# A decoder step with linear attention and window softmax: gate chain of the next tile moved into the output product, and scores as three half-precision passes

## What is computed

```
u = rmsnorm(x) * norm_in
gq, gk, gv, g_gate, g_low, sq, sk, sv, s_gate = split(u @ w_in)
log_a = log_sigmoid(g_low @ w_gate_up + b_gate) / 16           # per token and feature
o_gla[t] = q_t S_t,   S_t = diag(exp(log_a_t)) S_{t-1} + k_t v_t^T   # 4 heads of 64 x 128
p = softmax([q k^T / 8 over the last 128 tokens, sink])         # 8 query heads of 64, 2 key heads
o_swa = p v
y = rmsnorm(x + concat(rmsnorm(o_gla) * silu(g_gate), o_swa * silu(s_gate)) @ w_out) * norm_f
```

## Time and profile before

| | |
|---|---|
| median of 3 runs | 964.44 us (964.41 to 966.28) |
| the profiled execution | 965.73 us, span 963.9 us |
| PE busy | 890.4 us, 92% of the span |
| DVE busy | 693.7 us, 72% |
| ACT busy | 399.4 us, 41% |
| POOL busy | 98.4 us, 10% |
| mean granted clock of PE | 0.958 of 2.4 GHz |

### The profile page before, as it was taken

How to read it: one execution, slowest core, us unless ns; L and a number is a source line. 1 busy time by engine, 2 the same in 40 slices (tenths; PEclk the granted TensorE clock), 3 DMA queues, 4 the chain that set the end, 5 groups by cost and what they waited for, 6 DMA issues and landing times.

```text
span 963.9 us, 21703 instructions
## 1 busy us (share of the span) xinstructions
PE 890.4 (92%) x8701; PEld 619.6 (64%) x8701; DVE 693.7 (72%) x2124; ACT 399.4 (41%) x1096; POOL 98.4 (10%) x125
## 2 busy tenths in 40 slices
PE   1597689999999999999999999999999999999977
PEld 1583357585857667675758585766757575856755
DVE  5999858576685949585857768594958586776673
ACT  6786434343424344343434342434434343433311
POOL 1455101010100001010101010000101010101000
PEclk9799699999999999999999999999999999997776
DMA  9640102020202001020202020200102020101220
GB/s 378 239 176 1 66 1 88 1 90 1 89 1 88 3 35 54 1 89 1 89 1 89 1 88 1 89 2 33 58 2 88 1 89 1 48 2 45 80 109 24
DMA packets 15219, 56.47 MB, mean 59 GB/s; under 512 B 3569, under 2 KB 5001, under 8 KB 13840
## 3 DMA queue, kind: packets, MB, share of 16 engines
q1 hardware_dynamic: 14832, 55.02, 15.1%
q10 hardware_dynamic: 288, 0.07, 0.0%
HBM read 44.30 MB, written 10.78 MB: 57 GB/s over the span
## 4 chain that ended last, share of the span: by engine, by line
PE 71%; DVE 21%; ACT 3%; issue 3%; DMA 1%; SPq 0%; DVEq 0%
PE bank L516 19%; PE bank L517 18%; PE bank L518 18%; DVE flex L1413 4%; PE bank L667 3%; DVE bank L1407 2%; PE bank L601 2%; DVE flex L409 2%; PE bank L714 2%; PE bank L691 1%; PE bank L687 1%; DMA w_out_lo<-in_w 1%; DVE flex L1318 1%; PE bank L653 1%; DVE flex L408 1%
## 5 line engine op out<-in xcount | busy, mean ns | idle before, releaser
L516 PE MATMUL bank<-u_hi,w_in_hi_lo 128*128 128x128 f16 (+1 forms) x1288 | 209.7, 215 | 14.1 <-DVE w_in_hi_lo L1557 13.9
L517 PE MATMUL bank<-u_lo,w_in_hi_lo 128*128 128x128 f16 (+1 forms) x1288 | 209.4, 215 | 0.0
L518 PE MATMUL bank<-u_hi,w_in_hi_lo 128*128 128x128 f16 (+1 forms) x1288 | 209.4, 215 | 0.0
L516 PE MATMUL bank<-w_in_hi_lo,u_hi 128*128 128x512 f16 (+3 forms) x528 | 176.9, 343 | 1.1 <-ACT win_q L970 0.9
L517 PE MATMUL bank<-w_in_hi_lo,u_hi 128*128 128x512 f16 (+3 forms) x528 | 176.6, 343 | 0.0
L518 PE MATMUL bank<-w_in_hi_lo,u_lo 128*128 128x512 f16 (+3 forms) x528 | 176.6, 343 | 0.0
L516 PEld LDWEIGHTS bank<-u_hi,w_in_hi_lo 128*128 128x128 f16 x1288 | 124.6, 99 | 26.2 <-DVE w_in_hi_lo L1557 14.0
L517 PEld LDWEIGHTS bank<-u_lo,w_in_hi_lo 128*128 128x128 f16 x1288 | 124.5, 99 | 0.2
L518 PEld LDWEIGHTS bank<-u_hi,w_in_hi_lo 128*128 128x128 f16 x1288 | 124.5, 99 | 0.0
L516 PE MATMUL bank<-w_out_hi,ogT_hi 128*128 128x512 f16 x256 | 98.0, 383 | 0.0
L517 PE MATMUL bank<-w_out_lo,ogT_hi 128*128 128x512 f16 x256 | 98.0, 383 | 0.0
(11 more groups left out here) (270 smaller groups left out, 1811.1 us busy)
## 6 DMA issues: line engine op xcount, KB each, us to landing
xT<-in_xT SPq DMA_DIRECT2D x16, 512.0 KB, 4.5
x_rows<-in_xq SPq DMA_DIRECT2D x16, 512.0 KB
flex<-in_w SPq DMA_DIRECT2D x4, 2048.0 KB, 9.9
flex<-in_xq SPq DMA_DIRECT2D x16, 512.0 KB, 3.6
out_y<-flex SPq DMA_DIRECT2D x16, 512.0 KB, 2.6
w_out_lo<-in_w SPq DMA_DIRECT2D x2, 2048.0 KB, 10.1
w_out_hi<-in_w SPq DMA_DIRECT2D x1, 2048.0 KB, 10.2
w_out_hi<-in_w SPq DMA_DIRECT2D x1, 1088.0 KB, 7.2
```

What stands on the lines that cost most here:

```text
L516: nc.tensor.matmul(out, a_hi, b_hi, start=start and i == 0, stop=False)
L517: nc.tensor.matmul(out, a_hi, b_lo, start=False, stop=False)
L518: mm = nc.tensor.matmul(out, a_lo, b_hi, start=False, stop=stop and i == last)
```

## The change

Scores: queries and keys are kept as high and low 16-bit halves (`q16`, `k16`), and each score product is three half-precision matmuls that add up in PSUM (hi*hi, hi*lo, lo*hi). ACT writes the queries' high half from PSUM, DVE the low half (new `take_sq`), and DVE now frees the bank. DVE writes both halves of the keys. The scale is no longer applied to queries and keys but in `row_max`, where the immediate -1 becomes a per-partition scalar `nsig` made in the prologue. The keys to be returned are scaled apart (`k_last`).

Gate chain: of tile t+1 in iteration t. `turn_low` and `gate_up` stand before and behind the first part of `proj gg`; the order of the ring `tr` follows. `take_z` stands behind `take_gv`, `log_gate` behind `head_norm`, `sums` and then `split_v` behind `norm_x`, `decays` ahead of ACT's `split_u`, `factors` between `residual` and `final_norm`, POOL's `differences` at the end of its iteration. Tile 0 has its own copies of the first steps. In the last tile, ahead of which the sample tokens are projected, none of it is left. In the prologue ACT's `take_sq` of tiles 0 and 1 moves to rounds 3 and 4 and DVE gets its part in the same rounds.

```diff
         pj = Ring(banks[0:2], ...
-                  [("bc", "dve"), ("gqk", "act"), ("sq", "act"), ("sklow", "dve"), ("gv", "dve"),
+                  [("bc", "dve"), ("gqk", "act"), ("sq", "dve"), ("sklow", "dve"), ("gv", "dve"),
         tr = Ring(banks[4:6], ...
-                  [("glT", "act"), ("z", "dve"), ("pt0", "dve"), ("pt1", "dve"), ("pt2", "dve"), ("pt3", "dve"),
-                   ("KST", "act"), ("SU", "dve"), ("og0", "dve"), ("og1", "dve")])
+                  [("pt0", "dve"), ("pt1", "dve"), ("pt2", "dve"), ("pt3", "dve"), ("KST", "act"),
+                   ("glT", "act"), ("z", "dve"), ("SU", "dve"), ("og0", "dve"), ("og1", "dve")],
...
 # scores (PE)
                 for i in range(2):
-                    for h, name in enumerate(units):
-                        mm = nc.tensor.matmul(..., sq[r:r + HD, t.p, 2 * pair + i, :], kwin[r:r + HD, t.p, :],
-                                              start=True, stop=True)
+                    for step, (lq, lk) in enumerate(((0, 0), (0, 1), (1, 0))):
+                        for h, name in enumerate(units):
+                            mm = nc.tensor.matmul(..., q16[r:r + HD, t.p, lq, 2 * pair + i, :],
+                                                  k16[r:r + HD, t.p, lk, :], start=step == 0, stop=step == 2)
 # take_sq (ACT), take_sq (DVE, new)
+                    nc.scalar.activation(q16[:, t.p, 0], bank, ACT.Identity, scale=V_UNIT).then_inc(act_q.sem, 1)
+            def take_sq(t):
+                act_q.wait(dve, "qh", t)
+                V.scalar_tensor_tensor(out=q16[:, t.p, 1], in0=pj.bank("sq", t)[:, :].rearrange(
+                    "p (f c) -> p f c", f=GRP), scalar=V_UNIT, in1=q16[:, t.p, 0], op0=ALU.mult, op1=ALU.subtract
+                                       ).then_inc(pj.freed["dve"], 1)
 # take_kv (DVE)
-                    V.tensor_scalar(kwin[:, t.p, P:2 * P], bank[:, 0:P], inv[:, 2:3], None, ALU.mult)
+                    V.tensor_scalar(k[:, 0, P:2 * P], bank[:, 0:P], V_UNIT, None, ALU.mult).then_inc(dve_k.sem, 1)
                     V.tensor_scalar(vf[:, t.p, :], bank[:, P:2 * P], V_UNIT, None, ALU.mult)
+                    dve_k.wait(dve, "kh", t)
+                    V.scalar_tensor_tensor(out=k[:, 1, P:2 * P], in0=bank[:, 0:P], scalar=V_UNIT,
+                                           in1=k[:, 0, P:2 * P], op0=ALU.mult, op1=ALU.subtract)
 # row_max (DVE)
-                    m = V.tensor_tensor_reduce(..., band[:, first], -1.0,
+                    m = V.tensor_tensor_reduce(..., band[:, first], nsig[:, :],
 # PE, iteration
                 if not early:
-                    turn_low(t)
                     proj(nxt, "gqk")
-                    gate_up(t)
                     scores(t, 0)
...
                 turn_keys(t)
+                turn_low(t)
                 if early:
                     proj_rest(nxt, "gg", 6)
                 else:
                     proj(nxt, "gg", 3)
+                gate_up(t)
                 gla_out(t)
 # ACT, prologue and iteration
-                if i == 5:
-                    take_sq(Tile(1))
                 if i == 3:
                     take_qk(Tile(1))
+                    take_sq(Tile(0))
                 if i == 4:
-                    take_sq(Tile(0))
+                    take_sq(Tile(1))
...
-                decays(t)
                 probs(t, 2)
...
                 take_kst(t)
+                take_low(t)
                 head_norm(t)
+                log_gate(nxt)
                 take_out(t, 0)
...
                 nc.scalar.preload_act_table_set(LOG_EXP_SET)
+                decays(nxt)
                 split_u(t + 2)
 # DVE, prologue and iteration
+                    V.tensor_scalar(nsig[:, :], invq[:, 1:2], inv[:, 2:3], -1.0 / (V_UNIT * V_UNIT), ALU.mult, ALU.mult
+                                    ).then_inc(scored, 1)
+                    dve.wait_ge(scored, 1)
+                    V.tensor_scalar(nsig[:, :], nsig[:, :], -SCORE_FLOOR, None, ALU.min)
+                if i == 3:
+                    take_sq(Tile(0))
                 if i == 4:
+                    take_sq(Tile(1))
                     take_gv(Tile(0))
...
-                take_z(t)
                 row_max(t, 0)
                 row_max(t, 1)
-                sums(t)
+                take_sq(nxt)
                 take_pt(t, 0)
                 take_pt(t, 1)
                 row_max(t, 2)
                 row_max(t, 3)
-                factors(t)
                 take_pt(t, 2)
                 take_kv(nxt)
...
                 take_gv(nxt)
-                split_v(nxt)
+                take_z(t)
                 mean_square(t + 2)
                 gate_window(t)
...
                 norm_x(t + 2)
+                sums(nxt)
+                split_v(nxt)
                 scale_u(t + 2)
                 split_u(t + 2)
                 residual(t)
+                factors(nxt)
                 final_norm(t)
```

More of the change, by code:

```diff
@@ L114, with __init__ @@
 class Ring:
-    def __init__(self, banks, full, freed, order, tail=None, head=None):
+    def __init__(self, banks, full, freed, order, tail=None, head=None, last=None):
         self.banks, self.full, self.freed, self.order = banks, full, freed, order
+        self.last = order if last is None else last
         self.tail = order if tail is None else tail
@@ L126, in _list @@
     def _list(self, t):
+        if t.static and t.off == NT - 1:
+            return self.last
         return self.tail if t.sample else self.order
@@ L235, in hymba_step_kernel @@
         bsum = part(FT * P).rearrange("p (f c) -> p f c", f=FT)
+        KST = part(HG * DK)
+        k_last = part(P)
         assert at[0] <= 8192
@@ L616, in values @@
             def values(t, u):
-                if u == 0 and not (t.static and t.off == 0):
-                    dve_o.wait(pe, "sg", t + -1)
+                if u == 0:
+                    if t.static and t.off == 0:
+                        pe.wait_ge(z_taken, 1)
+                    else:
+                        dve_o.wait(pe, "sg", t + -1)
                 if u == 0:
@@ L643, in gate_up, with first_turn_low, first_gate_up @@
                 mm.then_inc(tr.full, 1)
+            def first_turn_low():
+                pj.wait_freed(pe, "sklow", Tile(0))
+                nc.tensor.transpose(accS[0:RANK, 0:P], glow[:, 0, :], ident[:, :]).then_inc(low_turned, 1)
+            def first_gate_up():
+                pe.wait_ge(low_taken, 1)
+                for f in range(FT):
+                    mm = nc.tensor.matmul(accS[:, (f + 1) * P:(f + 2) * P], wgu[:, f * P:f * P + P], glT[:, :],
+                                          start=True, stop=True)
+                mm.then_inc(z_full, 1)
             def leaf_scores(t):
@@ L969, in take_sq @@
                 bank = pj.bank("sq", t)[:, :].rearrange("p (f c) -> p f c", f=4)
-                nc.scalar.activation(sq[:, t.p, :, 0:n], bank[:, :, 0:n], ACT.Identity,
-                                     scale=invq[:, 1:2]).then_inc(pj.freed["act"], 1)
+                if t.sample:
+                    nc.scalar.activation(s_q[:, :, 0:n], bank[:, :, 0:n], ACT.Identity,
+                                         scale=invq[:, 1:2]).then_inc(pj.freed["act"], 1)
+                else:
+                    nc.scalar.activation(q16[:, t.p, 0], bank, ACT.Identity, scale=V_UNIT).then_inc(act_q.sem, 1)
             def take_gate(t, g):
@@ L1157, in body @@
                 early = t.static and t.off == 0
-                if not early:
-                    take_low(t)
+                if early:
+                    log_gate(t)
+                else:
                     take_qk(nxt)
-                log_gate(t)
                 probs(t, 0)
@@ L1175, in body @@
                     probs_hi(t, 1)
-                decays(t)
+                if early:
+                    decays(t)
                 probs(t, 2)
@@ L1746, in _ @@
                     dve.wait_ge(w_lo_pool, i)
-                    take_z(Tile(0))
+                    first_take_z()
                     row_max(Tile(0), 0)
@@ L1783, in body @@
                 early = t.static and t.off == 0
-                if not early:
-                    take_z(t)
+                if early:
+                    sums(t)
+                else:
                     row_max(t, 0)
                     row_max(t, 1)
-                sums(t)
+                if not early:
+                    take_sq(nxt)
                 take_pt(t, 0)
```

84 lines of the change are left out of this document (56 added, 28 removed).

## The result

The changed kernel takes **971.69 us** (median of 5 runs, 971.61 to 976.64) against 965.44 for the kernel before on the same chip: ratio 1.0088, interval 1.0074 to 1.0102. (The ratio takes in all runs, the two long ones too; the medians alone stand at 1.0065.) It is slower, as forecast, but by 6.2 us in the median instead of 2.6. 971.69 is within the outer range of 962.0 to 972.5, outside the forecast's own range of 964.5 to 970.5, and close to the 971.3 of rival (a).

A forecast was written before the change was run, and what follows sets the result against it. TensorE was taken as the bound, busy over nine tenths of the span; prologue +3.7, tile 0 +0.8, steady tiles -0.8 and tail -1.1 gave +2.6, 967.0 us as a median; own range 964.5 to 970.5, outer range 962.0 to 972.5.

The forecast's parts named there:

- rival (a): Prologue: PE's clock falls in the idle before gv of tile 1, +4.3 us more, 971.3 us; chance 0.2.
- The split takes the sums' place; the wait does not go: Steady tile, before the last transposes: DVE's query split replaces the sums; PE's wait grows about 0.45 to some 1.1 us.
- Rival (b): Steady tile: the wait goes after all, tile 51.1, 950 us; milder form 962.5; together chance 0.14.
- I take 0: Row maximum on DVE: a second per-partition scalar costs between 0 and 0.06 us per instruction, four on the path; taken as 0.
- One more change of rows: Steady tile, gate-up moved behind the hole on PE: one added change of rows, 0.09 us of the 0.84 moved.
- Cover enough by a hair: Tile boundary: ACT's second exponential ends at about 11.65, when PE asks for it at 11.69.
- Scores: Steady tile on PE: twelve half-precision matmuls with overlapping heads take 0.75 us, 0.31 less than before.
- Rival (d): Scores: the half-precision heads do not overlap, +9 us, 976 us; chance 0.06.
- Prologue +3.7: Prologue: DVE's split of tile 1's queries holds up PE's gv of tile 1, +3.7 us, bounds +1.1 and +8.5.
- Rival (c): Prologue: it hides its new work and PE's gv is not held up, 964.5 us; chance 0.10.
- Tile 0 +0.8: Tile 0: it takes gate-up of tile 1 on board, +0.8 us.
- Tail -1.1: Last tile, to the start of the sample's gv: 13.4 instead of 14.5 us, set by DVE, -1.1 us.

The follow-up runs named there:

- e2: Changed kernel with single-precision queries, keys and scores as before, so the gate chain's move alone: 965.64 us, ratio 1.0007.
- e1: Changed kernel with the immediate -1 back in the row maximum and the scores left without their scale: 969.89 us, ratio 1.0049.
- e9: Changed kernel with late query split, early leaf scores, prologue statements moved, scale in the query and key splits, immediate -1 in the row maximum: 947.86 us, ratio 0.9818.
- e4: Changed kernel with three prologue statements moved: ACT's tile 0 query copy later, DVE's tile 1 query split earlier: 968.45 us, ratio 1.0037.
- e3: Kernel before with the three-pass scores alone, gate chain in its old place, query split behind the sums: 1000.4 us, ratio 1.0367.
- e11: Kernel before with three-pass scores alone, query split behind the fourth row maximum on DVE and behind the probabilities on ACT: 990.52 us, ratio 1.0260.

## Why the prediction was right and where it failed

- **The split takes the sums' place; the wait does not go.** Right, and its size was close (1.15 us against "some 1.1"). The stretch that holds it came out 0.16 longer than forecast: 0.25 more for the row maxima, 0.09 less for ACT's copy. Rival (b) is out with it. What the forecast did not see is that before the change ACT's copy of the queries already stood just behind the sums, which e2 shows.
- **"I take 0" for the second per-partition scalar.** The step that failed. It measures 0.061 for each of the instructions, the upper bound that I had from the earlier trace rows. The reason given, that the instruction already fetches one, was an argument and no row. Four of them are on the path: 0.25 a tile, 3.4 us in all; taking the scalar away gave back 0.23 a tile (e1). The forecast's median was 4.7 us too low (3.6 in the difference to the kernel before), and this term is the greater part of it.
- **"One more change of rows" for gate-up.** It costs two, it seems: the scores kept theirs, and gate-up, once between `gqk` and the scores, now needs one on each side. `gg`'s three steps take 2.03 instead of 1.94, and the first matmuls of the output 0.97 instead of 0.86. 0.1 us a tile too little, 1.3 in all. No run isolates it. ACT's copy with an immediate scale (0.60 us, against 0.69 for the old one; e9 shows that it is the scale) gave back 0.09.
- **"Cover enough by a hair"** at the boundary: it was gone by a hair. The first four transposes take 0.69 us instead of 0.61; that costs nothing that shows in the changed kernel, but e9 shows that it counts once the hole is closed.
- **Scores** at 0.75 us with overlapping heads: 0.76. Rival (d) falls.
- **Prologue +3.7:** +3.9, by the waits named; only the bound step of DVE came at 82.99 instead of 80.2, as `gv` took longer. Rival (c) is out. **Tile 0 +0.8:** 1.0 without the clock. **Tail -1.1:** -0.56 to the sample's `gv` and -0.61 behind it, under other low stretches of the clock. With the same code there, e4's last tile takes 12.98 us instead of 13.85, 1.4 less than before, so this stage moves by 0.9 with the low stretches that fall into it.
- **Rival (a)** came true in the profiled run: 2.5 us instead of 4.3, as the clock came back during `gv`. What I held against it, that the fall in the earlier trace rows came late in its hole, was a poor argument from one case. That its 971.3 lies so near the median of 971.69 is luck: the account below reaches the median without that fall, by the tiles, and the profiled run, which has it, took 976.64. The rule of the Trainium skill ("TensorE: Matmul & The Clock Gate", the section on HAM oscillation), that idle gaps between bursts let the clock fall, agrees with the traces in the prologue: a fall in all seven profiles with the wait of 4.2 us or more, in none of the six without it.
- **Two sums in the rivals** do not come out of their own terms. 24 matmuls at 0.43 us instead of 0.22 are 5.0 us more and not 4.3, and with the 3.7 that makes 8.7, near the 8.5 given as the bound; rival (b)'s tile of 51.1 gives 951 and not 950.

Without the two low stretches before tile 1 the account is +2.6 as forecast, +3.7 from the tiles and +0.4 from all other stages, 6.7 (970.6 against 963.9); the medians are 6.2 apart. The +0.4 is a sum of four small misses that nearly cancel (+0.2, +0.2, +0.5, -0.6).

## What to carry to other kernels

When work leaves the front of a wait, ask who is second: here ACT's copy and then the split held the same wait, and the new order on DVE alone gave 0.32 us a tile, on ACT too another 0.26, and the early leaf scores on PE 0.75. Price an instruction's changed form by the unfavourable bound if it stands several times on the path, and count both borders of every stage that is moved. A step that nobody wants soon (the next tile's queries) belongs in the idle time behind the chain, and what has been made ready early (the leaf scores) in front of the wait: with the prologue's order and the scale moved back, that turned a ratio of 1.0088 into 0.9818.

## What the runs showed of the hardware

A row maximum with a second per-partition scalar took 405 ns, with an immediate 344 (e1). ACT's copy of 128x512 from PSUM to half precision took 0.69 us with a per-partition scale (e9) and 0.60 with an immediate one (the changed kernel). Waits have a price beyond their length: with 2.1 us of wait on PE in a tile the granted clock fell from 1.00 to 0.50 for 3.4 us in 13 of 14 tiles (e3), with 1.51 us ahead of the fall in 7 of 14 (e11), while with 1.15 us in the changed kernel it stayed at 1.00 through all 14. That is what went together; no run changed a wait and nothing else. A single wait of over 4 us in the prologue came with a fall in 7 profiles of 7. Why another low stretch near 129 to 141 us comes in some kernels and not in others stays open.
